# Hybrid convolution and pooling block on eight cores: norms of x in another order, a scrap buffer for their squares, and four multiplications by the norm vector on GpSimd

## The chip, the cores and the metric

The program runs on the 8 cores of one Trainium2 chip. Each core works alone on 2048 of the 16384 tokens (four sequences of 4096, two cores to a sequence) and on 32 tokens ahead of them, the halo; no core waits for another, though all read the same memory. The metric is the device time in microseconds (us) of the slowest core. Engines are named as the profile names them: PE (TensorE, matmuls), DVE (VectorE), ACT (ScalarE), POOL (GpSimd), SP (SyncE, which here only issues DMAs).

## The reference

Per token, with D = 1024 channels and all in float32:

```
u = rms_norm(x, mix_pre_g);  proj = u @ w_in                     # 1024 -> 5120
a, gate, p, g_conv, g_pool = split of proj in five
y_conv = silu(layer_norm(conv31(a * sigmoid(gate)))) @ w_conv_out # depthwise, causal
y_pool = (per_group_linear(pool(p), pool_w) * pool_scale) @ w_pool_out
h  = x + rms_norm((sigmoid(g_conv) * y_conv + sigmoid(g_pool) * y_pool) @ w_o, mix_post_g)
out = h + rms_norm(square(relu(rms_norm(h, mlp_pre_g) @ w_ff1)) @ w_ff2, mlp_post_g)
```

`pool` is, in each of four groups of 256 channels, a trailing mean over 2, 4, 8 or 16 tokens less the token itself. `rms_norm(x, g)` is x * rsqrt(mean(x*x) + eps) * g: a sum of squares per token, one factor per token, and a multiplication by the vector g.

## The kernel before

The kernel writes its instructions down in one fixed order, each onto the queue of its engine; every engine works its queue off in that order. A recording class (`KB`) notes which buffer each instruction reads and writes and puts semaphore waits where an instruction on another engine, or a DMA, has to be finished first. Nothing is reordered afterwards: an instruction that waits holds everything behind it on its engine.

**First stage, x and the pooling projection.** x comes in 16 tiles of 128 tokens (0 to 15) and the halo (-1), each 512 KB in float32, loaded by SP into nine staging buffers. `x_norm(j)`, written (nrm, j) in the list, normalises tile j: ACT squares it and sums along the row (`Square`, 128x1024; its by-product, the squares themselves, goes to the place where the normalised tile is going to lie, one of four buffers `xb`), ACT takes the root, DVE the reciprocal (L401), and DVE multiplies x by the factor and by the norm vector `gb0` in one SCALAR_TENSOR_TENSOR (L250, 128x1024, "STT" below) into bf16. Tiles 0 to 7 are then transposed on PE (`x_tr`, L223, eight 128x128 pieces, and DVE copies them from PSUM, L256, 128x8x128); tiles 8 to 15 by a DMA transpose that SP issues (`DTR`, L263). `p_unit(cc, u)`, written (pu, cc, u), is one group of 8 matmuls with 256 columns: channel chunk cc of the pooling projection for the tokens of tiles 2u and 2u+1; ACT (or DVE, for odd cc and u above 1) copies the result out of PSUM. The list in `do([...])` sets the order of all of these on all engines. After it come 16 groups with 512 columns (`p_group`) for tiles 8 to 11 and then 12 to 15, and the pooling itself on DVE, piece by piece. `wg_load` (POOL) fetches the weights of the next stage into slots 2 and 3 of the weight area, which hold nothing before that.

**Second stage, the gated convolution input.** Four quarters q, each with eight steps rp. A step `glu_pair(q, rp)` has 16 matmuls of 512 columns, a sigmoid on ACT and a multiplication on DVE (L241, 128x2x32x8). Beside them run the convolution's steps for the quarter before, in a cycle of four: three times `cv_w` on DVE (L246, 128x48x16, eight pieces in all, which write the one weight buffer `Wc`), then `cv_mm` on PE, 48 matmuls that read `Wc`, with two DVE additions. At the end of quarter 1 SP issues the load of `poolwT` (the group weights of the pooling branch, 1 MB) once the transposes of that quarter have ended (`cev[1]`). `weff_scale` multiplies it by `pool_scale` on DVE in eight instructions (L246, 128x256) at the end of quarter 2, and `weff_group` in quarter 3 multiplies the result with `w_pool_out` on PE. `pump(n)` takes up to n background tasks from a queue; the only ones in it in quarter 3 are 16 statistics (`BN_STATS`, L610) on DVE.

**Later stages** (gates, output projection, the MLP) take about 720 us and are not touched.

Of the kernel before, what the change touches and what calls it, by code (L numbers as in the profile page):

```python
# [7 lines left out]
F32 = mybir.dt.float32  # L8
BF16 = mybir.dt.bfloat16
AF = mybir.ActivationFunctionType  # L10
ALU = mybir.AluOpType
# [17 lines left out]
RW = TP + TP_N  # L29
SLOT = 4096  # L30
# [140 lines left out]
def build_program():  # L171
# [20 lines left out]
    with ExitStack() as es:  # L192
# [14 lines left out]
        def av(off, *dims, dt=BF16):  # L207
            n = int(np.prod(dims))
            v = arena[:, off:off + (n if dt is BF16 else 2 * n)]
            if dt is not BF16:  # L210
                v = v.bitcast(dt)
            if len(dims) > 1:
                names = ["d%d" % i for i in range(len(dims))]
                v = v.rearrange("p (" + " ".join(names) + ") -> p " + " ".join(names),
                                **{a: d for a, d in zip(names[:-1], dims)})
            return v
# [23 lines left out]
        def TTE(eng, o, a, b, op):  # L240
            kb.op(eng, lambda e: e.tensor_tensor(out=o, in0=a, in1=b, op=op), [a, b], [o])  # L241
# [6 lines left out]
        def STT(o, a, s, b, op0, op1):  # L248
            rd = [a, b] + ([] if isinstance(s, float) else [s])
            kb.op("dve", lambda e: e.scalar_tensor_tensor(out=o, in0=a, scalar=s, in1=b, op0=op0, op1=op1), rd, [o])  # L250
# [42 lines left out]
        c8 = lambda v: v.rearrange("p (k t) -> p k t", k=8)  # L293
        xst = [c8(av(o, 1024, dt=F32)) for o in (RW + 6 * SLOT, RW + 6 * SLOT + 2048, RW + 7 * SLOT, RS, RW + 4 * SLOT + 4192)]
        xst += [z[:, :, 1024 + 256 * i:1280 + 256 * i].bitcast(F32) for i in range(4)]
        gb0 = av(RW + 7 * SLOT + 2048, 1024, dt=F32)
        xb = [av(TP + 3584, 1024), av(TP + 4608, 1024), av(RS + 2048, 1024), av(RW + 4 * SLOT + 3168, 1024)]
        sig = [av(TP + 4160, 512, dt=F32), av(TP + 5184, 512, dt=F32)]
        s2b = [av(RW + 4 * SLOT + i * 1056, 528, dt=F32) for i in range(3)]
        identf = av(RW + 4 * SLOT + 2304, 128, dt=F32)  # L300
# [102 lines left out]
        def rstd(ssq_src, P, epsc, junk, eng):  # L403
            a, r = col()
            ACT(junk, ssq_src, AF.Square, scale=1.0 / 32, accum=a[:P])
            rsqrt(r[:P], a[:P], epsc, eng)
            return r[:P]
# [6 lines left out]
        def x_norm(j):  # L414
            i = x_order.index(j)
            P = 32 if j < 0 else 128
            src, dst = xst[x_buf[i]][:P], c8(xb[i % 4])[:P]
            r = rstd(src, P, 0, dst, "act")
            STT(dst, src, r, c8(gb0)[:P], ALU.mult, ALU.mult)
            if j >= 8:  # L420
                tev[j] = DTR(uT[:, :, H + 128 * j:H + 128 * (j + 1)], xb[i % 4])
            for n in range(9, len(x_order)):
                if x_buf[n] == x_buf[i] and n > i and x_order[n] not in xev:
                    x_load(x_order[n])
                    break
# [14 lines left out]
        def pump(n):  # L440
            for _ in range(n):
                if bgd:
                    bgd.popleft()()
# [74 lines left out]
        nrm, trn, pu, pg = x_norm, x_tr, p_unit, lambda cc, blk: p_group(cc, blk * 512, 512)  # L518
# [5 lines left out]
        def pads():  # L524
# [3 lines left out]
        do([(warm, 6), (nrm, 2), (setup,), (nrm, 3), (trn, 2), (warm, 3), (nrm, 0), (trn, 3), (nrm, 1), (nrm, -1), (warm, 14),  # L528
            (pu, 0, 1), (pu, 1, 1), (trn, 0), (trn, 1), (trn, -1), (pads,), (pu, 2, 1), (pu, 3, 1),
            (pu, 0, 0), (pu, 1, 0), (pu, 2, 0), (pu, 3, 0), (pu, 4, 1), (pu, 4, 0), (nrm, 4), (pu, 5, 1), (pu, 5, 0),  # L530
            (nrm, 5), (pu, 6, 1), (pu, 6, 0), (pu, 7, 1), (trn, 4), (pu, 7, 0), (trn, 5), (nrm, 6),
            (pu, 0, 2), (pu, 1, 2), (pu, 2, 2), (nrm, 7), (trn, 6), (pu, 3, 2), (pu, 4, 2), (nrm, 8), (pu, 5, 2),
            (trn, 7), (pu, 6, 2), (nrm, 9), (pu, 7, 2), (pu, 0, 3), (nrm, 10), (pu, 1, 3), (pu, 2, 3), (nrm, 11),
            (pu, 3, 3), (pu, 4, 3), (nrm, 12), (pu, 5, 3), (nrm, 13), (pu, 6, 3), (nrm, 14), (wg_load, 0), (pu, 7, 3),
            (nrm, 15), (wg_load, 1)])
        for blk in range(2):
            for cc in range(8):
                pq(cc, blk)
# [96 lines left out]
            for hh in range(2):  # L635
                WLOAD(wpo[hh], wpo_v[:, :, hh * 512:(hh + 1) * 512], after=[cev[1]])

        def weff_scale():
            for g in range(4):
                for jc in range(2):  # L640
                    if g == 0:
                        TS(pwT[:, g, jc, :], pwf[:, g, jc, :], vcol(16, 2 * g + jc), ALU.mult, 0.5, ALU.mult)
                    else:
                        TS(pwT[:, g, jc, :], pwf[:, g, jc, :], vcol(16, 2 * g + jc), ALU.mult)
# [11 lines left out]
        for q in range(4):  # L656
            glu_halo(q)
            steps = deque(conv_steps(q - 1) if q else [])
            for rp in range(8):
                glu_pair(q, rp)  # L660
                if steps:
                    steps.popleft()()
                pool_pump(1)
                pump(3)
                if q == 3 and rp % 2 == 0:
                    weff_group(rp // 2)
            conv_in(q)
            if q + 2 < 4:
                wg_load(q + 2)
            if q == 1:  # L670
                pool_pump(32)
                weff_prep()
            if q == 2:
                weff_scale()
                WLOAD(wgp, w_in_v[:, :, 4096:5120], after=[cev[2]])
            if q == 2:
                for r in range(16):
                    bgd.append(lambda r=r: ln_stat(0, r))
# [318 lines left out]
```

How the kernel before makes its waits and increments, by code:

```python
            def body(h, items=items):  # L156
                for waits, fn, ev, dma in items:
                    for sk, v in waits.items():
                        h.wait_ge(sems[sk], rank[sk][v] if sk in rank else v)
                    if fn is None:
                        continue
                    inst = fn(h)
                    if dma:
                        inst.then_inc(sems[ev[0]], 16)
                    elif ev[1] in rank[ev[0]]:
                        inst.then_inc(sems[ev[0]], 1)
```

## Time and profile before

| | us |
|---|---|
| median of 3 runs | 969.09 (968.52 to 1033.9) |
| the profiled execution | 967.8 |
| span of its slowest core (core 0), on which all rows below stand unless another core is named | 966.3 |
| spans of the other cores | 962.9 to 966.2 |
| PE busy in that span | 937.5 |
| DVE, ACT, POOL busy | 451.8, 287.9, 62.5 |
| TensorE's granted clock, mean | 0.997 of full |

The span runs from the first to the last instruction on the core; what the time has beyond it (1.5 us) is start and end. "Idle before, releaser" in a row is how long the engine had nothing to do before the row's first instruction, and which event ended it. A row that merges several instructions says how many (x24) and gives the time from the first start to the last end.

### The profile page before, as it was taken

What the parts mean: (1) busy time and instruction counts of PE and PEld (TensorE: products, weight loads), DVE (VectorE), ACT (ScalarE), POOL (GpSimd) and SP (SyncE); (2) the same over time, 40 slices, a digit from 0 to 9 for tenths busy, and PEclk for the clock granted to TensorE, in tenths of its full rate; (3) what the DMA queues carried; (4) which work ended last, traced back from release to release, by engine and by line L of the source; (5) the groups of instructions that cost most, each with busy time, mean ns of one, the idle gap of its engine ahead of it and who ended that gap; (6) DMA issues with size and microseconds to landing.
All of it is one profiled execution on the core that took longest, in us unless ns stands there. A gap on an engine that the chain in (4) does not pass through costs nothing.

```text
span 966.3 us, 13780 instructions; the slowest of 8 cores (962.9 to 966.3 us)
## 1 busy us (share of the span) xinstructions
PE 937.5 (97%) x4758; PEld 477.7 (49%) x4843; DVE 451.8 (47%) x767; ACT 287.9 (30%) x523; POOL 62.5 (6%) x112
## 2 busy tenths in 40 slices
PE   8889999999999999999999999999999999999996
PEld 4655666665544444444444444444444444444444
DVE  5478786575482134565666620444213431244222
ACT  4553111132115922333335520233112321133211
POOL 1010001000010000121222100000000000000000
PEclk9999999999999999999999999999999999999998
DMA  9986165966894623578879993310022001210021
GB/s 181 256 137 88 27 80 106 144 99 105 116 145 73 123 89 49 128 149 199 154 185 184 211 181 58 131 44 1 1 88 88 1 1 44 88 43 1 1 87 66
DMA packets 109750, 95.39 MB, mean 99 GB/s; under 512 B 60241, under 2 KB 91217, under 8 KB 109554
## 3 DMA queue, kind: packets, MB, share of 16 engines
q0 software_dynamic: 32416, 35.13, 26.4%
q1 hardware_dynamic: 77266, 59.38, 23.5%
q8 instruction: 40, 0.66, 0.3%
q14 instruction: 28, 0.23, 0.1%
HBM read 98.88 MB, written 16.84 MB: 120 GB/s over the span
## 4 chain that ended last, share of the span: by engine, by line
PE 90%; DMA 3%; DVE 2%; ACT 2%; issue 2%; DVEq 0%; ACTq 0%; SPq 0%
PE ps L220 90%; ACT arena L238 2%; DMA arena<-w_in 2%; DMA arena<-xh 1%; DVE arena L241 1%; DVE arena L246 1%; DVE arena L250 0%; PE ps L223 0%; DVE arena L478 0%; ACT sm L238 0%; ACTq L159 0%; DVEq L159 0%; DVE ps L241 0%; DVE arena L256 0%; DVEq L192 0%
## 5 line engine op out<-in xcount | busy, mean ns | idle before, releaser
L220 PE MATMUL ps<-arena 128*128 128x512 bf16 (+4 forms) x4646 | 931.4, 360 | 17.8 <-ACT arena L238 4.7
L220 PEld LDWEIGHTS ps<-arena 128*128 128x128 bf16 (+1 forms) x4731 | 470.6, 103 | 473.8 <-issue 24.5
L238 ACT ACTIVATE arena<-ps 128x512 bf16<-128x512 f32 (+5 forms) x346 | 202.8, 593 | 606.0 <-PE ps L220 450.4
L246 DVE TENSOR_SCALAR ps<-ps 128x512 f32<-128x512 f32 x128 | 89.1, 699 | 110.9 <-PE ps L220 110.3
L241 DVE TENSOR_TENSOR ps<-ps,arena 128x512 f32<-128x512 f32 (+1 forms) x65 | 43.6, 688 | 177.2 <-ACT arena L238 176.7
L250 DVE SCALAR_TENSOR_TENSOR arena<-arena,ps 128x512 bf16<-128x512 f32 (+1 forms) x64 | 43.7, 686 | 126.1 <-ACT arena L238 126.1
L241 DVE TENSOR_TENSOR arena<-ps,arena 128x512 bf16<-128x512 f32 (+2 forms) x52 | 42.3, 830 | 35.5 <-ACT arena L238 29.4
L238 ACT ACTIVATE arena<-arena 128x1024 bf16<-128x1024 f32 (+1 forms) x33 | 34.8, 1054 | 44.6 <-DVE arena L250 35.8
L250 DVE SCALAR_TENSOR_TENSOR arena<-ps,sm,arena 128x512 f32<-128x512 f32 (+1 forms) x65 | 45.1, 737 | 4.1 <-DVE sm L401 3.3
L250 DVE SCALAR_TENSOR_TENSOR arena<-arena,sm 128x1024 bf16<-128x1024 f32 (+1 forms) x33 | 42.3, 1282 | 4.3 <-POOL sm L397 2.4
L241 DVE TENSOR_TENSOR arena<-arena 128x512 bf16<-128x512 f32 (+2 forms) x56 | 38.4, 690 | 4.3
L238 ACT ACTIVATE arena<-arena,vec 128x2048 bf16<-128x2048 bf16 x8 | 31.3, 3918 | 1.7 <-DMA arena<-arena 1.7
L246 DVE TENSOR_SCALAR arena<-arena,vec 128x768 bf16<-128x768 bf16 (+1 forms) x72 | 28.2, 420 | 2.7
L266 POOL DMA_DIRECT2D arena<-w_in x14 | 12.6, 908 | 157.6 <-DMA arena<-arena 138.1
L266 POOL DMA_DIRECT2D arena<-w_ff x16 | 13.5, 851 | 99.5 <-PE ps L220 92.4
L610 DVE BATCH_NORM_STATS2 bnst<-arena 128x6 f32<-128x512 bf16 x32 | 19.9, 680 | 0.0
L397 POOL TENSOR_TENSOR sm<-sm,mhalf 128x1 f32<-128x1 f32 x32 | 18.1, 567 | 5.0 <-POOL sm L396 0.4
L401 DVE RECIPROCAL sm<-sm 128x1 f32<-128x1 f32 (+1 forms) x33 | 5.3, 162 | 27.2 <-ACT sm L238 16.4
L250 DVE SCALAR_TENSOR_TENSOR arena<-arena 128x512 bf16<-128x512 f32 x24 | 16.5, 687 | 1.2
L478 DVE TENSOR_TENSOR_SCAN arena<-arena,scr 128x512 f32<-128x512 f32 x12 | 15.3, 1278 | 2.3 <-ACT arena L238 2.3
L396 POOL TENSOR_SCALAR sm<-sm 128x1 f32<-128x1 f32 x32 | 7.1, 221 | 133.0 <-DVE sm L241 67.6
L238 ACT ACTIVATE sm<-sm,epst 128x1 f32<-128x1 f32 (+1 forms) x33 | 9.7, 295 | 16.1 <-DVE sm L241 14.5
(34 smaller groups left out, 90.8 us busy)
## 6 DMA issues: line engine op xcount, KB each, us to landing
arena<-xh SPq DMA_DIRECT2D x32, 512.0 KB, 8.3
arena<-w_ff POOLq DMA_DIRECT2D x16, 1024.0 KB, 27.4
out<-arena SPq DMA_DIRECT2D x31, 512.0 KB, 2.9
arena<-out SPq DMA_DIRECT2D x16, 512.0 KB, 4.1
arena<-w_in POOLq DMA_DIRECT2D x12, 512.0 KB, 14.4
arena<-w_in POOLq DMA_DIRECT2D x2, 2048.0 KB, 17.9
arena<-gb SPq DMA_DIRECT2D x4, 512.0 KB, 7.0
arena<-w_pool_out POOLq DMA_DIRECT2D x2, 1024.0 KB, 23.7
```

Source lines behind the costliest of these rows:

```text
L220: kb.op("pe", lambda e: e.matmul(o, lhsT=l, rhs=r, start=start, stop=stop), [l, r], [o])
L238: kb.op("act", lambda e: e.activation(out=o, in_=i, func=func, **kw), rd, wr)
L241: kb.op(eng, lambda e: e.tensor_tensor(out=o, in0=a, in1=b, op=op), [a, b], [o])
L246: kb.op("dve", lambda e: e.tensor_scalar(out=o, in0=a, scalar1=s1, scalar2=s2, op0=op0, **kw), rd, [o])
L250: kb.op("dve", lambda e: e.scalar_tensor_tensor(out=o, in0=a, scalar=s, in1=b, op0=op0, op1=op1), rd, [o])
L266: return kb.op("pool", lambda e: e.dma_start(out=o, in_=src), [], [o], dma=True, after=after)
L396: kb.op("pool", lambda e: e.tensor_scalar(out=o, in0=i, scalar1=EPS[epsc], scalar2=None, op0=ALU.add), [i], [o])
L397: kb.op("pool", lambda e: e.tensor_tensor(out=o, in0=o, in1=mhalf[:, 0:n], op=ALU.pow), [o, mhalf[:, 0:n]], [o])
L401: kb.op("dve", lambda e: e.reciprocal(o, o), [o], [o])
L478: kb.op("dve", lambda e: e.tensor_tensor_scan(so, pc[:, lo:lo + n], pc[:, lo - w:lo - w + n], init, ALU.add, ALU.subtract), rd, [so])
L610: kb.op("dve", lambda e: e.bn_stats(o, i), [i], [o])
```

## The change

`x_norm` writes the squares to two scrap buffers `junk` in slot 2 of the weight area, no longer to the place of the normalised tile. For tiles 8, 10, 12 and 14 POOL multiplies x by `gb0` into one of two float32 buffers `xgs` (slots 2 and 3), and DVE multiplies that by the factor per token with a TENSOR_SCALAR. The list has (nrm, 6) to (nrm, 15) one to three entries earlier, and the two `wg_load` behind the last group. `weff_scale` takes a group: its eight instructions move from the end of quarter 2 into steps 1, 3, 5 and 7 of that quarter, two each. `pump(3)` becomes `pump(2)`.

```diff
+        junk = [av(RW + 2 * SLOT + i * 1024, 1024) for i in range(2)]
+        xgs = [c8(av(RW + 2 * SLOT + 2048 + i * 2048, 1024, dt=F32)) for i in range(2)]
...
             src, dst = xst[x_buf[i]][:P], c8(xb[i % 4])[:P]
-            r = rstd(src, P, 0, dst, "act")
-            STT(dst, src, r, c8(gb0)[:P], ALU.mult, ALU.mult)
+            if j in (8, 10, 12, 14):
+                xg = xgs[j // 2 % 2]
+                TTE("pool", xg, src, c8(gb0), ALU.mult)
+                TS(dst, xg, rstd(src, P, 0, c8(junk[i % 2]), "act"), ALU.mult)
+            else:
+                STT(dst, src, rstd(src, P, 0, c8(junk[i % 2])[:P], "act"), c8(gb0)[:P], ALU.mult, ALU.mult)
...
-            (nrm, 5), (pu, 6, 1), (pu, 6, 0), (pu, 7, 1), (trn, 4), (pu, 7, 0), (trn, 5), (nrm, 6),
-            (pu, 0, 2), (pu, 1, 2), (pu, 2, 2), (nrm, 7), (trn, 6), (pu, 3, 2), (pu, 4, 2), (nrm, 8), (pu, 5, 2),
-            (trn, 7), (pu, 6, 2), (nrm, 9), (pu, 7, 2), (pu, 0, 3), (nrm, 10), (pu, 1, 3), (pu, 2, 3), (nrm, 11),
-            (pu, 3, 3), (pu, 4, 3), (nrm, 12), (pu, 5, 3), (nrm, 13), (pu, 6, 3), (nrm, 14), (wg_load, 0), (pu, 7, 3),
-            (nrm, 15), (wg_load, 1)])
+            (nrm, 5), (pu, 6, 1), (pu, 6, 0), (pu, 7, 1), (trn, 4), (nrm, 6), (pu, 7, 0), (trn, 5),
+            (pu, 0, 2), (nrm, 7), (pu, 1, 2), (trn, 6), (pu, 2, 2), (nrm, 8), (pu, 3, 2), (pu, 4, 2), (trn, 7), (nrm, 9), (pu, 5, 2),
+            (pu, 6, 2), (nrm, 10), (pu, 7, 2), (pu, 0, 3), (nrm, 11), (pu, 1, 3), (nrm, 12), (pu, 2, 3), (pu, 3, 3), (nrm, 13),
+            (pu, 4, 3), (pu, 5, 3), (nrm, 14), (pu, 6, 3), (nrm, 15), (pu, 7, 3), (wg_load, 0), (wg_load, 1)])
...
-        def weff_scale():
-            for g in range(4):
+        def weff_scale(g):
...
                 pool_pump(1)
-                pump(3)
+                if q == 2 and rp % 2 == 1:
+                    weff_scale(rp // 2)
+                pump(2)
...
             if q == 2:
-                weff_scale()
                 WLOAD(wgp, w_in_v[:, :, 4096:5120], after=[cev[2]])
```

The order on DVE in the first stage, from the STT of tile 5 to the copy of tile 6's transposes (128x1024 is a norm's multiplication, 128x8x128 the copy of a tile's transposes out of PSUM, 128x256 that of a group of matmuls). Before:

```order
L250 SCALAR_TENSOR_TENSOR arena<-arena,sm 128x1024
L256 COPY arena<-ps 128x8x128 x2
L401 RECIPROCAL sm<-sm 128x1
L250 SCALAR_TENSOR_TENSOR arena<-arena,sm 128x1024
L256 COPY arena<-ps 128x256
```

Now:

```order
L250 SCALAR_TENSOR_TENSOR arena<-arena,sm 128x1024
L256 COPY arena<-ps 128x8x128
L403 RECIPROCAL sm<-sm 128x1
L250 SCALAR_TENSOR_TENSOR arena<-arena,sm 128x1024
L256 COPY arena<-ps 128x8x128
```

The copies of tiles 4 and 5 stood next to each other; now the STT of tile 6 stands between them, ahead of the copy of tile 5.

The order on DVE in quarter 2 of the second stage, steps rp = 1 to 3 (128x2x32x8 ends a `glu_pair`, 128x48x16 is `cv_w`, 128x16x64 the additions behind `cv_mm`, 128x256 `weff_scale`). Before:

```order
L241 TENSOR_TENSOR arena<-ps,arena 128x2x32x8
L246 TENSOR_SCALAR arena<-arena,vec 128x48x16 x3
L241 TENSOR_TENSOR arena<-ps,arena 128x2x32x8
L246 TENSOR_SCALAR arena<-arena,vec 128x48x16 x2
L241 TENSOR_TENSOR arena<-ps,arena 128x2x32x8
L241 TENSOR_TENSOR arena<-ps,arena 128x16x64 x2
```

Now:

```order
L241 TENSOR_TENSOR arena<-ps,arena 128x2x32x8
L246 TENSOR_SCALAR arena<-arena,vec 128x48x16 x3
L246 TENSOR_SCALAR arena<-arena,vec 128x256 x2
L241 TENSOR_TENSOR arena<-ps,arena 128x2x32x8
L246 TENSOR_SCALAR arena<-arena,vec 128x48x16 x2
L241 TENSOR_TENSOR arena<-ps,arena 128x2x32x8
L241 TENSOR_TENSOR arena<-ps,arena 128x16x64 x2
L246 TENSOR_SCALAR arena<-arena,vec 128x256 x2
```

The first two scalings of `poolwT` now stand in step 1, ahead of the last two `cv_w` for which `cv_mm` waits; before, all eight stood behind step 7.

The order on POOL from the start of the program (w_in is the weight of the first and then of the second stage). Before:

```order
L266 DMA arena<-w_in 128x8x256 x8
L266 DMA arena<-convw 128x768 x2
```

Now:

```order
L266 DMA arena<-w_in 128x8x256 x4
L241 TENSOR_TENSOR arena<-arena 128x1024 x4
L266 DMA arena<-w_in 128x8x256 x4
```

The four multiplications by `gb0` stand ahead of the four loads of `wg_load`.

## Rows read from the trace of the kernel before

**Rows 1.** Busy time by engine in the first stage (us, PE, PEld, DVE, ACT, POOL).

```profile
18.00:60.00 42.00, 34.55 (x322) 28.63 (x324) 22.74 (x42) 24.95 (x61) 0.00 (x0) 1.00 1.00 212
```

**Rows 2.** Timeline of PE, first stage: start, us, what, [idle before, releaser].

```profile
34.84 0.61 PE L223 MATMUL ps<-identb,arena 128*128 128x128 bf16 x8 [1.39 <-ACT arena L238]
...
38.07 2.78 PE L220 MATMUL ps<-arena 128*128 128x256 bf16 x24 [1.05 <-ACT arena L238]
...
44.55 0.61 PE L223 MATMUL ps<-identb,arena 128*128 128x128 bf16 x8 [0.64 <-DVE arena L250]
...
47.99 7.15 PE L220 MATMUL ps<-arena 128*128 128x256 bf16 x64 [1.08 <-ACT sm L238]
58.02 42.29 PE L220 MATMUL ps<-arena 128*128 128x512 bf16 x191 [2.88 <-ACT arena L238]
```

**Rows 3.** Load of tile 8: SP's issue, then size and us from issue to landing.

```profile
30.50 1.30 SPq L259 DMA_DIRECT2D arena<-xh  x1
...
arena<-xh SPq DMA_DIRECT2D x1, 512.0 KB, 7.2
```

**Rows 4.** Timeline of ACT: three evictions; the Squares of tiles 6 and 7.

```profile
34.41 0.92 ACT L238 ACTIVATE arena<-ps 128x256 f32<-128x256 f32 x3
...
36.77 1.05 ACT L238 ACTIVATE arena<-arena 128x1024 bf16<-128x1024 f32 x1
...
41.23 1.05 ACT L238 ACTIVATE arena<-arena 128x1024 bf16<-128x1024 f32 x1
```

**Rows 5.** Timeline of DVE: copy of tile 5's transposes; STTs of tiles 6 and 11.

```profile
37.13 0.69 DVE L256 COPY arena<-ps 128x1024 bf16<-128x1024 bf16 x1 [0.36 <-PE ps L223]
...
38.66 1.28 DVE L250 SCALAR_TENSOR_TENSOR arena<-arena,sm 128x1024 bf16<-128x1024 f32 x1
...
53.09 1.28 DVE L250 SCALAR_TENSOR_TENSOR arena<-arena,sm 128x1024 bf16<-128x1024 f32 x1
```

**Rows 6.** DMA transposes of tiles 8 and 11: issue, and us to landing of each.

```profile
46.88 1.52 SPq L263 DMA_TRANSPOSE arena<-arena  x1
...
54.51 1.23 SPq L263 DMA_TRANSPOSE arena<-arena  x1
...
arena<-arena SPq DMA_TRANSPOSE x1, 6.4
...
arena<-arena SPq DMA_TRANSPOSE x1, 3.1
```

**Rows 7.** Load of poolwT: SP's issue on core 0; landing on cores 0 and 1.

```profile
161.42 0.38 SPq L259 DMA_DIRECT2D arena<-poolwT  x1
...
arena<-poolwT SPq DMA_DIRECT2D x1, 1024.0 KB, 7.2
...
arena<-poolwT SPq DMA_DIRECT2D x1, 1024.0 KB, 5.2
```

**Rows 8.** Timeline of DVE, quarter 2: step 1, cv_w in step 2, weff_scale.

```profile
161.57 0.69 DVE L241 TENSOR_TENSOR arena<-ps,arena 128x512 bf16<-128x512 f32 x1 [1.58 <-ACT arena L238]
162.18 1.75 DVE L246 TENSOR_SCALAR arena<-arena,vec 128x768 bf16<-128x768 bf16 x3
...
165.63 0.94 DVE L246 TENSOR_SCALAR arena<-arena,vec 128x768 bf16<-128x768 bf16 x2
...
188.20 2.18 DVE L246 TENSOR_SCALAR arena<-arena,vec 128x256 bf16<-128x256 f32 x8
```

**Rows 9.** Chain that ended last, quarter 2: last matmuls of step 3 before cv_mm.

```profile
164.60 2.98 PE ps L220 x13
```

**Rows 10.** POOL: groups by shape (xcount | busy us, mean ns); an issue in quarter 2.

```profile
L396 POOL TENSOR_SCALAR sm<-sm 128x1 f32<-128x1 f32 x32 | 7.1, 221 | 133.0 <-DVE sm L241 67.6 <-ACT arena L238 65.3
...
L397 POOL TENSOR_TENSOR lnr<-lnr,mhalf 128x16 f32<-128x16 f32 x1 | 2.9, 2942 | 0.1
...
L396 POOL TENSOR_SCALAR lnr<-bnag 128x16 f32<-128x16 f32 x1 | 0.3, 269 | 20.0 <-DVE bnag L705 20.0
...
161.92 1.85 POOL L266 DMA_DIRECT2D arena<-w_in  x2 [12.15 <-DMA arena<-arena]
```

## The prediction, made before the changed kernel had run

> **What bounds the kernel now.** The table of the page comes first: PE is busy 937.5 of 966.3 us, so 28.8 us are all that any reordering can win. The busy time by stretch then says where to look. From 18 to 60 us PE works 34.55 of 42.00 us [rows 1], so a quarter of all the idle time lies in the stretch whose list is rewritten. PE's timeline splits that up: waits of 1.39, 1.05, 0.64, 1.08 and 2.88 us, together 7.04 [rows 2]. The reader should see what each is for, which the releaser named does not always say. At 34.84 PE waits for the norm of tile 4. At 38.07 it waits for DVE's copy of tile 5's transposes, which ends at 37.13 + 0.69 = 37.82 [rows 5]. At 44.55 it waits for the norm of tile 7, at 47.99 for the copy of that tile's transposes. At 58.02 the releaser is given as ACT, but the first group of 512 columns reads tiles 8 to 11, and the DMA transpose of tile 11 lands at 54.51 + 3.1 = 57.61 [rows 6]: 0.41 us later PE starts. In quarter 2 of the second stage PE has no wait that matters; there the views to read are DVE's timeline and SP's, because an instruction is moved there ahead of others.
>
> **First part: the list of the first stage.** Tile 4's norm stays where it is, so the 1.39 us stay. Tile 6's moves up, past the last eviction of (pu, 7, 0) and past the copy of tile 5's transposes. Its Square now follows the three evictions that end at 34.41 + 0.92 = 35.33, instead of starting at 36.77; from a Square to its STT are 38.66 - 36.77 = 1.89 us [rows 4, 5]. So the STT of tile 6 starts at 37.2 and ends at 38.5. The copy of tile 5, ready at 37.13 before, now stands behind it: 38.5 to 39.2. PE started 0.25 us after the copy, so it resumes at 39.4 instead of 38.07: **1.3 us lost**.
>
> From 38.07 to 47.99 + 7.15 = 55.14 PE worked 17.07 us less the two waits of 0.64 and 1.08, that is 15.35 [rows 2]. Both waits go. The Square of tile 7 follows the eviction of (pu, 0, 2): 39.4, a group of 0.93 (2.78 / 3 [rows 2]), about 0.6 for the copy out of PSUM: 41.0, hardly before the 41.23 of rows 4. Its STT ends near 44.2, and PE comes to tile 7's transposes only at 44.55 - 0.64 + 1.3 = 45.2. The copy of these transposes stood behind the STT of tile 8, now stands ahead of the STT of tile 9, and is done by 47; PE wants it at 47.99 - 1.72 + 1.3 = 47.6. So PE reaches the groups of 512 columns at 39.4 + 15.35 = 54.8, and what ends last is again the transpose of tile 11. The Square of tile 11 follows the eviction of (pu, 0, 3): 47.6 + 0.9 + 0.65 = 49.2. The STT is at 51.1 to 52.4, the transpose is issued at 52.5, lands at 55.6 if it takes 3.1 us, and PE starts at 56.0. That is one end. The other: the transpose of tile 8 took 6.4 us and landed at 53.3 [rows 6] because loads of x were still coming in; the next three, now issued closer together, can follow only as fast as SP issues them, 1.23 us each, and the last lands at 57.0, PE at 57.4. I take 56.4, nearer to the first, since tile 11's issue, at 52.5, comes 5.6 us after 46.88, more than 3 x 1.23. **Gain 1.6 us, between 0.6 and 2.0.**
>
> **Second part: POOL's four multiplications.** No row shows a plain two-operand multiplication on POOL. From above, the power of 128x16 took 2.942 us, which for 1024 elements would be 188 us; from below, 128x16 with one tensor took 0.269 us. Nearest is the slope of that simple operation, (0.269 - 0.221) / 15 = 3.2 ns an element [rows 10], so 3.5 us each, an estimate. The Trainium skill (GPSIMD Engine Reference, Elementwise — side-by-side cycle accounting) measures 4497 ns for an addition of 2048 elements, by which it would be 2.25 us and the sum would be the same. Tile 8 lands at 30.50 + 7.2 = 37.7 [rows 3]; its product is wanted near 45, tile 10's near 49, tile 14's near 56. So up to 4.5 us each is covered. DVE's remaining TENSOR_SCALAR costs between 0.27 us (the 128x256 of rows 8) and the 1.28 of an STT; up to 1 us is saved on each of four, off PE's path but for tiles 8 and 10. The scrap buffers take away ACT's wait for the old contents of `xb`; the same wait moves to DVE, for the transpose of four tiles before, which costs PE nothing, since those STTs only feed transposes needed eight groups, 14.2 us, later. `wg_load` stands behind the multiplications on POOL, but waits for the transpose of tile 13 anyway: nothing.
>
> **Third part: weff_scale.** The first two of its eight scalings move from behind step 7 into step 1 of quarter 2. The load of `poolwT` is issued by SP at 161.42 and lands 7.2 us later, at 168.62 [rows 7]; before, its first reader ran at 188.20 and never waited. In step 1 DVE is through with `cv_w` at 162.18 + 1.75 = 163.93 [rows 8]. Now it **waits there 4.7 us** for the load, and an in-order engine holds everything behind: the scalings (2 x 2.18 / 8 = 0.55), the multiplication of step 2 (0.61) and the two last `cv_w` (0.94). These end at 170.7 and PE can start `cv_mm` at 171.0, where it started at 164.60 + 2.98 = 167.6 [rows 9]. **Cost 3.4 us**, and PE, busy almost all of the rest, cannot win it back. Everything here moves with PE, the load included, since the load is released by the transposes at the end of quarter 1; the gain of the first part does not change the gap. The lower end is none; with the 5.2 us that the load takes on core 1 [rows 7] it would be 1.4. The upper is the forecast's own, unless the load slows down further. I take 3.4, since the slowest core sets the time. The other six scalings find the load landed. What leaves the end of quarter 2 (2.18 us of DVE) had PE work beside it: nothing. `pump(2)` for `pump(3)` gives the sixteen statistics 8 x 2 places instead of 8 x 3, just enough: nothing.
>
> **Sum.** Against the profiled execution: 967.8 - 1.6 + 3.4 = 969.6. The median of the runs stands 1.3 above that execution, so **970.9**: no change by the 2% (19.4 us) that a measurement of this kernel can tell. Its own range, from the ends of the first part: 970.5 to 971.9.
>
> **The rivals.**
> - *The load of poolwT comes early enough.* For it: 5.2 us on core 1. Against: 7.2 on core 0, the slowest. With 1.4 us the time is 968.9, with no wait 967.5. Chance 0.24, of which 0.04 for 966.2, where PE does not lose the 1.3 us at the copy of tile 5 either.
> - *POOL and DVE get in each other's way.* Beside POOL's DMA issues at 161.92, three `cv_w` on DVE took 1.75 us where two took 0.94 [rows 8, 10], so 0.3 more than their share. If each multiplication on POOL takes turns with the STT beside it, the STTs of tiles 6 and 11, both on PE's path, take 1.2 us more each: the transpose of tile 11 lands at 58.0, PE starts at 58.4, and the time is 967.8 + 0.4 + 3.4 + 1.3 = 972.9. If the STT waits out a multiplication of 3.5 us, it is 5 us instead of 2.4, and 975.5. Chance 0.18. The Trainium skill (GPSIMD Engine Reference, Specifications) has POOL share its SBUF interfaces with DVE, with contention for DVE instructions with two SBUF inputs, as an STT is; the row of `cv_w` agrees for a one-input instruction, and none shows an STT beside a multiplication.
> - *POOL's multiplication is slow enough to be the bound: slower.* PE wants tiles 12 to 15 eight groups of eight matmuls after 56.4, at 56.4 + 64 x 42.29 / 191 = 70.6 [rows 2]. With T us each the fourth product is there at 37.7 + 4T, the last transpose some 5.5 us later. PE waits for it from T = 6.8 on, and the kernel is slower by 2% (17.6 us more than in my sum) from T = 11.3. For it: the power's 184 ns an element. Against: the simple operation's 3.2. Chance 0.02.
> - *The norms do not follow the loads.* Tile 8 had landed at 37.7, yet tile 7's Square still stands behind an eviction that PE releases near 41. This is in my sum; if the transposes' queue takes the rest, the gain is 0.6 and the time 971.9.
>
> **How the numbers follow.** Forecast 0.55; load early 0.24; contention 0.18; slow POOL 0.02; something else 0.01. From 967.2 to 974.5 the range holds the forecast, most of the first rival and two thirds of the second. Faster by over 2% needs two thirds of all idle time: 0.01. Slower by over 2% is POOL's rival: 0.02. Within: 0.97.
>
> **What would show it.** On PE: the wait near 38 grows to 2.4, those near 44 and 48 go, the first group of 512 columns starts near 56.4. On DVE: a wait of 4 to 5 us for the load of `poolwT` in step 1 of quarter 2; on PE, 3 us before `cv_mm` near 169. POOL: four rows of 2 to 4.5 us. Without DVE's wait the third part is wrong; with STTs over 1.5 us beside POOL, the second.

## The result, and the profile after

The changed kernel takes **975.65 us** (median of 4 runs, 973.32 to 995.71; the kernel before 968.81 beside it). The ratio is 1.0065 with a 95% interval of [1.0041, 1.0089]: 0.65% or 6.3 us slower, which is more than the measurement is uncertain, though less than 2%. The prediction had 970.9 and a range to 974.5. The profiled execution took 975.57 us. One run of each of the two kernels (995.71 and 1033.9) fell into a second, slower state of the chip; all ratios, and the medians under the experiments, leave such runs out.

The cores fall apart. The marks in this table are the sigmoids of the 32 halo tokens that open each quarter of the second stage (a 32x256 row on ACT): the first mark ends the first stage, and from the third to the fourth is quarter 2. The waits are those of DVE for the load of `poolwT` and of PE before the next `cv_mm`; the clock is the granted one, in the slices of 5 us named.

| core | span before / after | first mark before / after | quarter 2 before / after | DVE / PE wait | clock 170-175, 175-180 |
|---|---|---|---|---|---|
| 0 | 966.3 / 966.0 | 88.97 / 89.78 | 34.98 / 36.3 | 2.42 / 1.15 | 1.00, 1.00 |
| 1 | 964.3 / 973.6 | 88.88 / 92.10 | 34.98 / 40.9 | 5.85 / 4.16 | 1.00, .66 |
| 2 | 966.2 / 965.7 | 90.57 / 89.50 | 34.99 / 36.4 | 2.54 / 1.24 | 1.00, 1.00 |
| 3 | 964.0 / 974.0 | 88.89 / 92.52 | 34.98 / 41.2 | 4.54 / 3.42 | .83, .50 |
| 4 | 964.2 / 971.3 | 89.38 / 92.52 | 34.98 / 38.8 | 5.34 / 3.66 | 1.00, 1.00 |
| 5 | 962.9 / 968.1 | 87.89 / 91.39 | 34.99 / 36.5 | 2.48 / 1.37 | 1.00, 1.00 |
| 6 | 965.2 / 972.5 | 89.71 / 90.98 | 34.98 / 41.0 | 5.37 / 4.26 | .98, .68 |
| 7 | 964.6 / 972.2 | 88.83 / 90.59 | 34.98 / 40.9 | 5.74 / 4.15 | .88, .78 |

Core 3, now the slowest, lost 10.0 us: 3.6 in the first stage (88.89 to 92.52), 6.25 in quarter 2, and 0.2 in quarter 1. The change has two costs where a gain and a smaller cost were forecast.

**The first stage on core 3.** PE (start, us, what, [idle before, releaser]), the rows that answer to [rows 2]:

```profile
35.22 0.68 PE L223 MATMUL ps<-identb,arena 128*128 128x128 bf16 x8 [0.47 <-ACT arena L238]
38.08 1.91 PE L220 MATMUL ps<-arena 128*128 128x256 bf16 x16 [2.18 <-DVE arena L256]
...
45.04 0.61 PE L223 MATMUL ps<-identb,arena 128*128 128x128 bf16 x8 [1.99 <-ACT sm L238]
45.49 9.77 PE L220 MATMUL ps<-arena 128*128 128x256 bf16 x88
58.72 11.65 PE L220 MATMUL ps<-arena 128*128 128x512 bf16 x41 [3.46 <-DMA arena<-arena]
```

The wait near 38 grew to 2.18 and the one near 48 went, both as forecast. But the one near 44 is longer, 1.99, and the 512-column groups start at 58.72 instead of the forecast 56.4 (on this core they started at 56.24 before). The reason stands in POOL's and DVE's timelines of the same core:

```profile
41.35 2.35 POOL L241 TENSOR_TENSOR arena<-arena 128x1024 f32<-128x1024 f32 x1 [1.20 <-DMA arena<-xh]
46.79 2.36 POOL L241 TENSOR_TENSOR arena<-arena 128x1024 f32<-128x1024 f32 x1 [3.09 <-DVE arena L246]
51.65 2.36 POOL L241 TENSOR_TENSOR arena<-arena 128x1024 f32<-128x1024 f32 x1 [2.49 <-DVE arena L246]
```

```profile
35.94 1.28 DVE L250 SCALAR_TENSOR_TENSOR arena<-arena,sm 128x1024 bf16<-128x1024 f32 x1
...
41.39 3.40 DVE L250 SCALAR_TENSOR_TENSOR arena<-arena,sm 128x1024 bf16<-128x1024 f32 x1
...
47.75 2.49 DVE L250 SCALAR_TENSOR_TENSOR arena<-arena,sm 128x1024 bf16<-128x1024 f32 x1
...
50.75 0.75 DVE L246 TENSOR_SCALAR arena<-arena,sm 128x1024 bf16<-128x1024 f32 x1
51.42 0.42 DVE L256 COPY arena<-ps 128x256 f32<-128x256 f32 x1
...
52.01 3.08 DVE L250 SCALAR_TENSOR_TENSOR arena<-arena,sm 128x1024 bf16<-128x1024 f32 x1
```

An STT with no multiplication beside it still takes 1.28 us, as in [rows 5]. The three that overlap one (tiles 7, 9 and 11) take 3.40, 2.49 and 3.08, and each ends 1.08 or 1.09 us after POOL does (44.79 against 43.70, 50.24 against 49.15, 55.09 against 54.01): nearly its whole length lies behind POOL's. POOL's first multiplication, from 37.79 to 40.14, has no STT beside it. Over the cores the STT of tile 9 takes 2.48 to 2.78 and that of tile 11 3.08 or 3.09; that of tile 7 is back at 1.29 on core 7, where it starts ahead of the multiplication. The STT of tile 7 makes PE wait at 45.04, that of tile 11 delays the last transpose. The Trainium skill (GPSIMD Engine Reference, Specifications) has such contention for DVE instructions with two SBUF inputs; the trace agrees, and has the size: 1.2 to 2.1 us more for each. The wait goes both ways, and the one that starts second has it. On core 6 POOL's first multiplication starts while an STT runs; the STT keeps its 1.28, and the multiplication takes 3.12 (POOL, then DVE):

```profile
36.39 3.12 POOL L241 TENSOR_TENSOR arena<-arena 128x1024 f32<-128x1024 f32 x1 [30.86 <-DMA arena<-xh]
```

```profile
36.02 1.28 DVE L250 SCALAR_TENSOR_TENSOR arena<-arena,sm 128x1024 bf16<-128x1024 f32 x1
```

**The clock behind that wait, and quarter 2.** Busy time by engine on core 3 (us, PE, PEld, DVE, ACT, POOL, granted clock, DMA share, GB/s), before and then after:

```profile
55.00:85.00 30.00, 28.76 (x127) 12.76 (x128) 23.70 (x46) 11.55 (x21) 3.50 (x4) 0.94 0.83 126
150.00:190.00 40.00, 40.00 (x275) 27.67 (x273) 23.78 (x43) 5.53 (x10) 4.70 (x6) 1.00 0.96 148
```

```profile
55.00:85.00 30.00, 26.54 (x113) 11.37 (x111) 21.57 (x46) 10.13 (x20) 3.56 (x4) 0.89 0.91 132
150.00:190.00 40.00, 36.14 (x225) 25.55 (x224) 22.73 (x42) 4.56 (x8) 4.66 (x6) 0.91 0.85 132
```

Of core 3's 3.6 us in the first stage, 2.5 are the later start of the 512-column groups and 1.1 come behind it, where the clock over 55 to 85 us was 0.94 and is 0.89. In 150 to 190 us PE now stands idle for 3.86 us, where before it never did, and its clock falls to 0.91. Closer, the load of `poolwT` (SP's issue and its time to landing), then DVE, then PE behind it, all on core 3:

```profile
164.81 0.38 SPq L259 DMA_DIRECT2D arena<-poolwT  x1
...
DMA to landing us min/median/max: 7.2/7.2/7.2
```

```profile
165.69 1.95 DVE L246 TENSOR_SCALAR arena<-arena,vec 128x768 bf16<-128x768 bf16 x3
172.18 0.62 DVE L246 TENSOR_SCALAR arena<-arena,vec 128x256 bf16<-128x256 f32 x2 [4.54 <-DMA arena<-poolwT]
172.71 0.68 DVE L241 TENSOR_TENSOR arena<-ps,arena 128x512 bf16<-128x512 f32 x1
173.31 0.94 DVE L246 TENSOR_SCALAR arena<-arena,vec 128x768 bf16<-128x768 bf16 x2
```

```profile
174.50 7.68 PE L220 MATMUL ps<-arena 128*128 128x128 bf16 x58 [3.42 <-DVE arena L246]
```

Landing at 164.81 + 7.2 = 172.0, a wait of 4.54 on DVE, of 3.42 on PE: the forecast was 4.7 and 3.4. What the forecast lacked comes after it. The clock of three slices, from the wait on:

```profile
170.00:175.00 5.00, 1.58 (x11) 0.97 (x10) 2.56 (x6) 0.60 (x1) 0.20 (x1) 0.83 1.18 191
175.00:180.00 5.00, 5.00 (x46) 4.74 (x45) 1.34 (x2) 0.00 (x0) 0.36 (x1) 0.50 1.25 140
180.00:185.00 5.00, 5.00 (x24) 3.36 (x23) 2.25 (x5) 0.60 (x1) 0.00 (x0) 0.99 1.20 164
```

PE comes back and works a whole slice at 0.50, the lower of its two levels (1.2 of 2.4 GHz). Half the work of 5 us is 2.5 us; with 3.42 of waiting and about 0.3 (an estimate) for the 0.5 us that PE had worked before 175, at 0.50 too, that makes the 6.25. The table shows it on every core: quarter 2 is longer than 34.98 by the PE wait and 0.2 more where the clock stays at 1.00 (cores 0, 2, 4, 5), and by the wait and 1.8 more on cores 1, 6 and 7, 2.8 on core 3, where it falls. Only on core 3 does it fall while PE still waits; on cores 1, 6 and 7 it falls some 0.6 to 1.1 us after PE has come back. On core 1 PE resumes at 174.87, still has 0.99 in the first of these slices, and works the next three us at 0.50:

```profile
175.00:176.00 1.00, 1.00 (x21) 1.00 (x20) 0.22 (x1) 0.00 (x0) 0.56 (x1) 0.99 1.25 140
176.00:179.00 3.00, 3.00 (x32) 3.00 (x30) 1.23 (x1) 0.00 (x0) 0.00 (x0) 0.50 1.20 126
```

The Trainium skill (TensorE: Matmul & The Clock Gate, HAM oscillation — how this bites in real kernels) tells of matmuls that restart at the half clock after a wait for a DMA; the trace agrees on core 3 and, with that delay, on cores 1, 6 and 7, while core 4, with a wait of 3.66 us, kept its clock.

### The profile page after: what moved, and what is told of

Its sections match the earlier page's. It is cut to its first block, busy times and chain, and to the rows that moved or that the text cites. A ratio compares the mean times of both kernels' runs of the same rounds, so it can differ in the third digit from the quotient of the medians.

```text
span 974.0 us, 13877 instructions; the slowest of 8 cores (965.7 to 974.0 us)
## 1 busy us (share of the span) xinstructions
PE 944.8 (97%) x4843; PEld 479.5 (49%) x4843; DVE 454.5 (47%) x767; ACT 287.8 (30%) x523; POOL 71.8 (7%) x116
## 4 chain that ended last, share of the span: by engine, by line
PE 89%; DMA 5%; DVE 3%; issue 1%; ACT 1%; DVEq 0%; POOL 0%; ACTq 0%; SPq 0%
PE ps L220 89%; DMA arena<-w_in 2%; DMA arena<-xh 1%; DVE arena L246 1%; DMA arena<-arena 1%; ACT arena L238 1%; DMA arena<-poolwT 1%; DVE arena L250 1%; DVE arena L484 0%; DVE arena L241 0%; PE ps L223 0%; ACT sm L238 0%; DVE arena L256 0%; POOL arena L266 0%; DVEq L159 0%
```

## The experiments

Ratios are to the kernel before, run on the same chip beside each, with 95% intervals. "First mark" is that of the table; means are over the eight cores of one profiled execution.

**a1_weff_back: the change without its third part.**

```diff
-                if q == 2 and rp % 2 == 1:
-                    weff_scale(rp // 2)
...
             if q == 2:
+                for g in range(4):
+                    weff_scale(g)
```

> The change with weff_scale back at the end of quarter 2; list, scrap buffers and POOL's multiplications stay. Theory of two losses: DVE does not wait for poolwT, so PE has no wait in quarter 2 and its granted clock stays at 1.00 there; quarter 2 takes 35.0 us on every core, as before (36.3 to 41.2 with the change). The first stage stays late: first group of 512 columns at 58 to 59.7, STTs of tiles 7, 9 and 11 at 2.5 to 3.4 us. Time about 971 (968.8 + 2 to 3). Rival, that the first stage's lateness is what makes the second stage lose (the load of poolwT or the clock suffers from it): quarter 2 stays at 36 to 41 us and the time near 975.

Measured 1.0019 [1.0004, 1.0033]; profiled 969.86. Quarter 2 is back at 35.0 us on all cores and the clock there at 1.00, so the moved scalings are the whole of what was lost in quarter 2. The first stage stays as in the change: the 512-column groups start at 58.3 to 59.4, the first mark is 91.15 on the mean (before 89.14).

**a2_no_pool_mult: the change without POOL's multiplications** (tiles 8, 10, 12, 14 by STT like the others).

```diff
-            if j in (8, 10, 12, 14):
+            if j in ():
```

> The change without POOL's four multiplications (all tiles by the STT); list, scrap buffers and the moved weff_scale stay. Theory of two losses: all STTs take 1.28 us again, the transpose of tile 11 lands near 56 and the first group of 512 columns starts at 56.4, 2 us earlier than with the change; quarter 2 still takes 36 to 41 us. Time about 972 (975.6 less 2 to 4, the more where the clock also stays up after the shorter wait). Rival, that the list itself makes the first stage late (tile 6's norm ahead of the copy of tile 5): the first group stays at 58 or later and the time at 975.

Measured 1.0046 [1.0029, 1.0063], median 972.2. All STTs take 1.28 or 1.29 again, on every core; the one of tile 11 on core 3:

```profile
49.70 1.28 DVE L250 SCALAR_TENSOR_TENSOR arena<-arena,sm 128x1024 bf16<-128x1024 f32 x1
```

The 512-column groups start at 54.9 to 57.5 and the first mark comes at 86.0 to 89.5, so the late start was POOL's doing. Quarter 2 takes 36.5 to 41.1 us as in the change; the clock fell on cores 0 and 6 this time, not on 1, 3, 6 and 7.

**a3_weff_alone: the kernel before, with the third part only.**

```diff
+                if q == 2 and rp % 2 == 1:
+                    weff_scale(rp // 2)
...
-                weff_scale()
```

> The kernel before with nothing but weff_scale moved into steps 1, 3, 5 and 7 of quarter 2. Theory of two losses: first stage as before, quarter 2 at 36 to 41 us instead of 35.0, with a wait of PE of 1 to 4 us before cv_mm and on some cores half the granted clock behind it. Time 973 to 974 (968.8 + 5). If the load of poolwT landed late only because the first stage was late: no wait, 968.8.

Measured 1.0063 [1.0045, 1.0081], 973.9 us: as slow as the whole change, from eight small instructions. PE waits 1.4 to 4.1 us. Cores 1, 2 and 5 worked on at a lower clock; here PE on core 2 and two slices of its clock:

```profile
172.65 9.66 PE L220 MATMUL ps<-arena 128*128 128x128 bf16 x68 [3.82 <-DVE arena L246]
```

```profile
170.00:175.00 5.00, 2.35 (x23) 2.38 (x24) 2.56 (x6) 0.00 (x0) 0.56 (x1) 0.61 1.21 137
175.00:180.00 5.00, 5.00 (x39) 4.20 (x37) 2.97 (x4) 0.00 (x0) 0.00 (x0) 0.71 1.20 158
```

Core 2's quarter 2 takes 41.5 us: 34.98, 3.8 of waiting, 2.7 more.

**b3_fill_the_wait: a3, with 14 matmuls of 512 columns whose result nothing reads in front of the `cv_mm` that waits.** If the lower clock is a cost of its own, added work in the wait should win it back.

```diff
             if cc == 2:
+                b = banks(2)
+                for _ in range(14):
+                    MM(ps[:, b, :], uT[:, 0, H:H + 128], uT[:, 0, H:H + 512], True, True)
...
```

> The kernel before with weff_scale moved into steps 1, 3, 5 and 7 (as a3_weff_alone), and 14 matmuls of 512 columns, 3.0 us, whose result nobody reads, in front of the cv_mm that waits. PE then does not stand still for more than about 1 us there. Theory that the granted clock falls because PE stood still for 3.3 us and more: clock 1.00 in quarter 2 on all cores, quarter 2 at 38.0 us where the wait was shorter than 3.0 and 38.4 to 39.1 where it was 3.4 to 4.1, time 972 (974.2 with the wait empty), although work was added. Rival, that the clock falls for another reason (the loads running beside it): some cores at half the clock as in a3_weff_alone, quarter 2 up to 41 us, time 974.

Measured 1.0048 [1.0034, 1.0062], 972.4: 3.0 us more work on PE (quarter 2 takes 38.0 on cores 1, 3, 5 and 7, where the wait is covered), and yet no slower than a3; the 1.5 us less by the ratios are not shown, since the two intervals overlap. The clock in quarter 2 is 1.00 on all cores. On cores 0, 2, 4 and 6 PE would have stood still for 3.5 to 5.0 us without the filler (filler and remaining wait together); a2, a3 and the change have twelve unfilled waits of 3.3 us and more in quarter 2, and nine of them were followed by the lower clock. Core 4 has a wait left, behind its filler, and keeps its clock too (PE, then the clock):

```profile
174.05 8.25 PE L220 MATMUL ps<-arena 128*128 128x128 bf16 x72 [2.01 <-DVE arena L246]
```

```profile
175.00:180.00 5.00, 4.94 (x49) 3.93 (x48) 2.97 (x4) 0.00 (x0) 0.02 (x1) 1.00 1.25 151
```

The slowest quarter 2 falls from 41.5 to 40.2 us. So the fall of the clock comes from PE's wait, and is paid on top of it.

**b2_weff_steps_4_to_7: the scalings in the loop, but later** (in b1 below, one group in each of steps 4 to 7).

```diff
+                if q == 2 and rp >= 4:
+                    weff_scale(rp - 4)
```

> As b1_tile6_back, but with weff_scale spread over the steps of quarter 2 as in the change, one group in each of steps 4, 5, 6 and 7 in place of 1, 3, 5 and 7. The load of poolwT lands at 165 to 171, step 4 asks at about 175. Theory that the wait for the load is the whole cost of the move: no wait of DVE or PE, quarter 2 at 35.0 us, granted clock 1.00 there, time as b1_tile6_back within 0.5 us. Rival, that DVE's work in the steps delays cv_w and the multiplications by itself: quarter 2 longer than 35.5 us and the time 1 us or more above b1_tile6_back.

Measured 0.9994 [0.9984, 1.0003]. DVE waits for no load, quarter 2 is 35.0 us and its clock 1.00 on all cores. Interleaving costs nothing; standing ahead of the load costs all of it.

**a4_list_and_scrap: the change without its second and third parts** (new list, scrap buffers, `pump(2)`).

```diff
-            if j in (8, 10, 12, 14):
+            if j in ():
...
-                if q == 2 and rp % 2 == 1:
-                    weff_scale(rp // 2)
...
+                for g in range(4):
+                    weff_scale(g)
```

> The change with weff_scale back at the end of quarter 2 and without POOL's multiplications: what is left is the new list, the scrap buffers and pump(2). By my prediction's first part: 1.3 us lost at the copy of tile 5, both waits near 44 and 48 gone, first group of 512 columns at 56.4, quarter 2 at 35.0; time 967.2 (968.8 - 1.6). Rival, that the list is itself a loss: 970 or more.

Measured 0.9987 [0.9977, 0.9997], 966.5: **faster than both kernels**, by 1.3 us against the kernel before, where 1.6 was forecast. PE on core 0, to be read against [rows 2]:

```profile
38.05 3.51 PE L220 MATMUL ps<-arena 128*128 128x256 bf16 x16 [2.18 <-DVE arena L256]
...
44.97 9.77 PE L220 MATMUL ps<-arena 128*128 128x256 bf16 x88
56.74 13.54 PE L220 MATMUL ps<-arena 128*128 128x512 bf16 x61 [2.00 <-ACT arena L238]
```

The waits near 44 and 48 are gone, the one near 38 is 2.18, the 512-column groups start at 56.74 (55.2 to 57.7 over the cores; forecast 56.4). The first mark is 87.87 on the mean, 1.27 earlier.

The longer wait near 38 has a second cost, for which the forecast has no term. Behind it the same 16 matmuls take 3.51 us on core 0 (above) and 1.91 on core 3:

```profile
38.20 1.91 PE L220 MATMUL ps<-arena 128*128 128x256 bf16 x16 [2.18 <-DVE arena L256]
```

The clock over 37 to 43 us is 0.72 or 0.73 on cores 0, 2 and 4 and 1.00 on the others; in the change it is 0.72 on cores 1, 2, 4, 5 and 6, in the kernel before on core 6 alone. That core 0 starts so near to the forecast is therefore partly chance: it came to the transposes of tile 4, whose place no part of the change moves, at 33.60, and at 34.84 in [rows 2]. Counted from there the 512-column groups start after 22.6 us on the mean over the cores, before after 23.4.

**b1_tile6_back: a4 with the norm of tile 6 back behind (trn, 5)**, to win the 1.3 us at the copy of tile 5.

```diff
-            (nrm, 5), (pu, 6, 1), (pu, 6, 0), (pu, 7, 1), (trn, 4), (nrm, 6), (pu, 7, 0), (trn, 5),
+            (nrm, 5), (pu, 6, 1), (pu, 6, 0), (pu, 7, 1), (trn, 4), (pu, 7, 0), (trn, 5), (nrm, 6),
```

> The list and the scrap buffers alone (POOL's multiplications and the moved weff_scale undone) with tile 6's norm back behind the transposes of tile 5. If the STT of tile 6 ahead of the copy of tile 5 costs PE what the changed kernel shows (a wait of 2.2 us near 38 where it was 1.05), the wait goes back to about 1 us, all that follows in the first stage, paced by PE, is 1.2 us earlier, and the time is 966 (967.0 - 1.2). If the DMA transpose of tile 11 is what ends last whatever PE does before it, PE only waits longer at its first group of 512 columns, and the time stays at 967.

Measured 0.9996 [0.9986, 1.0005], 967.3. The wait near 38 is back at 1.05 us, the clock behind it is 1.00 on all cores, and counted from the transposes of tile 4 the 512-column groups start after 21.4 us, 1.2 sooner than in a4. But PE pays it out there: it still waits for the transpose of tile 11, now 1.8 to 3.5 us, and on five cores (two in a4) the clock of 55 to 85 us is .94 or .95. The first mark is 87.82 on the mean, that of a4 87.87. Core 5:

```profile
37.71 1.91 PE L220 MATMUL ps<-arena 128*128 128x256 bf16 x16 [1.05 <-ACT arena L238]
...
55.41 14.80 PE L220 MATMUL ps<-arena 128*128 128x512 bf16 x60 [2.29 <-DMA arena<-arena]
```

```profile
55.00:85.00 30.00, 29.59 (x129) 12.95 (x130) 23.59 (x46) 9.33 (x18) 3.59 (x5) 0.94 0.87 123
```

**c1_fill_first_stage: b1 with ten unread matmuls of 512 columns in that wait.**

```diff
+            if (cc, t0) == (0, 1024):
+                b = banks(1)
+                for _ in range(10):
+                    MM(ps[:, b, :], uT[:, 0, H:H + 128], uT[:, 0, H:H + 512], True, True)
...
```

> As b1 (967.41, ratio 0.9996), with ten matmuls of 512 columns whose result nothing reads (about 2.2 us at full clock) on PE in front of the first group of 512 columns. In b1 PE waits 1.8 to 3.5 us there and the granted clock of 55 to 85 us is .94 on six cores. Theory (part of the list's gain is lost to the clock that falls after this wait): the ten matmuls lie in the wait, the clock of 55 to 85 us is 1.00 on all cores, halo(0) ends between 86 and 87.5 us on all cores instead of 85.7 to 90.0, and the time is about 966, ratio 0.997 to 0.999. Rival (the clock at 55 to 85 us has another cause, or the fill is simply work that is added): the same clock as b1 and 0 to 2.2 us more, 967.4 to 969.6.

Measured 0.9987 [0.9978, 0.9997], 966.2. The clock of 55 to 85 us is 1.00 on seven cores (in b1 on three; the six with .94 that the expectation names are five), and the first mark comes at 85.4 to 88.2 on those seven; core 3, where 2.37 us of waiting were left, has .94 and 89.69. On core 5 PE starts the real work 0.66 us later than in b1 and ends the stage 1.03 us earlier (87.23 against 88.26). That fits the theory, though it is one profiled execution of each; that the time is lower than b1's is not shown, since the intervals overlap. Core 5 again:

```profile
56.07 14.19 PE L220 MATMUL ps<-arena 128*128 128x512 bf16 x65 [1.13 <-DMA arena<-arena]
```

```profile
55.00:85.00 30.00, 28.93 (x134) 13.07 (x135) 24.04 (x47) 9.64 (x17) 4.61 (x6) 1.00 0.83 125
```

**c2_norms_earlier: b1 with the norms of tiles 7 to 11 earlier still.**

```diff
-            (pu, 0, 2), (nrm, 7), (pu, 1, 2), (trn, 6), (pu, 2, 2), (nrm, 8), (pu, 3, 2), ...
+            (nrm, 7), (pu, 0, 2), (pu, 1, 2), (trn, 6), (nrm, 8), (pu, 2, 2), (pu, 3, 2), ...
```

> As b1, with the norms of tiles 7 to 11 one or two groups of matmuls earlier still. Theory (the first group of 512 columns waits for the transpose of tile 11, whose issue follows its norm): the group starts 1 to 2 us earlier than in b1, and the time is 966 to 966.5. Rival (the loads of x and the transposes' queue limit the transposes, not the norms): the group starts where it does in b1, within 0.5 us on the median core, and the time is that of b1, 967.4.

Measured 0.9991 [0.9982, 1.0001], 966.3. The 512-column groups start at 54.7 to 56.3, in b1 at 54.2 to 57.2, with a median that is the same within 0.2. The rival holds: nothing is to be seen of a gain from moving these norms further.

**b4_all_eight_on_pool: a1 with tiles 8 to 15 all multiplied on POOL.** No STT is left beside a multiplication then, only TENSOR_SCALARs, which read one tensor. I expected these to be spared; the rival had every DVE instruction on SBUF wait.

```diff
-            if j in (8, 10, 12, 14):
-                xg = xgs[j // 2 % 2]
+            if j >= 8:
+                xg = xgs[j % 2]
```

> The change with weff_scale back at the end of quarter 2 and all of tiles 8 to 15 multiplied by the norm vector on POOL, so that behind tile 7 no STT runs beside a multiplication, only the TENSOR_SCALAR with one tensor input. Theory that only an instruction with two SBUF inputs waits out POOL's multiplication: TENSOR_SCALAR 0.75 us throughout, STT of tile 7 at 2 to 3.4 us (the only one), first group of 512 columns at 57, time 968 (between a4_list_and_scrap's 967.0 and a1_weff_back's 969.9). Rival, that every DVE instruction on SBUF waits, the one-input ones too: TENSOR_SCALAR at 1.5 to 3 us, first group at 59 or later, time 970 or more.

Measured 1.0035 [1.0018, 1.0053]. **My theory fell.** POOL and then DVE on core 6:

```profile
52.61 2.37 POOL L241 TENSOR_TENSOR arena<-arena 128x1024 f32<-128x1024 f32 x1 [0.70 <-DVE arena L246]
```

```profile
45.61 0.75 DVE L246 TENSOR_SCALAR arena<-arena,sm 128x1024 bf16<-128x1024 f32 x1
...
52.39 0.41 DVE L256 COPY arena<-ps 128x256 f32<-128x256 f32 x1
...
52.98 2.55 DVE L246 TENSOR_SCALAR arena<-arena,sm 128x1024 bf16<-128x1024 f32 x1
55.45 0.41 DVE L256 COPY arena<-ps 128x256 f32<-128x256 f32 x1
```

A TENSOR_SCALAR of 0.75 us takes 2.55 beside POOL and ends 0.55 after it. The copies out of PSUM keep 0.41, beside POOL or not. The change has one such on core 7, of 1.66 us. The Trainium skill (GPSIMD Engine Reference, Specifications) names, beside DVE instructions with two SBUF inputs, those that run in a mode with two ports. That this TENSOR_SCALAR runs in one would fit its 0.75 us against the STT's 1.28; no row names the mode.

**c3_scrap_alone: the kernel before with the scrap buffers only.** The first `wg_load` still stands ahead of the norms of tiles 14 and 15, so their squares overwrite weights that the next stage multiplies with.

```diff
+        junk = [av(RW + 2 * SLOT + i * 1024, 1024) for i in range(2)]
...
-            r = rstd(src, P, 0, dst, "act")
-            STT(dst, src, r, c8(gb0)[:P], ALU.mult, ALU.mult)
+            STT(dst, src, rstd(src, P, 0, c8(junk[i % 2])[:P], "act"), c8(gb0)[:P], ALU.mult, ALU.mult)
```

> The kernel before with one thing of the change: the squares' by-product goes to the two scrap buffers. Theory (ACT's wait for the old contents moves to DVE and neither is on PE's path): no change, ratio 0.999 to 1.001. Rival (ACT's wait did hold a tile's norm on PE's path): 1 us faster or more, ratio under 0.999.

A miss by my own edit: its profiled spans are 970 to 977 us and no ratio is drawn from it. ACT's square of tile 14 waits for the weights to land in its scrap buffer, and PE then waits 6.49 us for the transposes of the last tiles (core 0, ACT, then PE):

```profile
72.87 1.06 ACT L238 ACTIVATE arena<-arena 128x1024 bf16<-128x1024 f32 x1 [15.67 <-DMA arena<-w_in]
```

```profile
79.60 25.62 PE L220 MATMUL ps<-arena 128*128 128x512 bf16 x105 [6.49 <-DMA arena<-arena]
```

It shows why the change has the two loads behind the last norm.

**c4_scrap_loads_behind: c3 with the two loads there.**

```diff
-            (pu, 3, 3), (pu, 4, 3), (nrm, 12), (pu, 5, 3), (nrm, 13), (pu, 6, 3), (nrm, 14), (wg_load, 0), (pu, 7, 3),
-            (nrm, 15), (wg_load, 1)])
+            (pu, 3, 3), (pu, 4, 3), (nrm, 12), (pu, 5, 3), (nrm, 13), (pu, 6, 3), (nrm, 14), (pu, 7, 3),
+            (nrm, 15), (wg_load, 0), (wg_load, 1)])
```

> The kernel before with the two scrap buffers, and the two loads of the next stage's weights behind the last norm, as the change has them (in c3 the first of them stood ahead of the norms of tiles 14 and 15, whose squares went into the slots that it fills, and the end of the first halo moved from 88 to 91 us to 95 to 102 us). Theory (the scrap buffers and the place of the loads are off PE's path): the first halo ends between 87.5 and 91 us as before, and the time is that of before, ratio 0.999 to 1.001. Rival (the loads come later and the next stage waits for its weights): the first halo ends 2 us or more later and the ratio is 1.002 or more.

Measured 1.0006 [0.9996, 1.0016]: no change. The gain of a4 is the list's; `pump(2)`, which a4 has too, acts only behind the first stage.

## Why the prediction was wrong

By the ratios, times 968: list and buffers -1.3 us (a4), POOL's multiplications +3.1 (a1 less a4), the scalings +4.5 (change less a1) to +6.1 (a3 alone). With 4.5 the sum is the measured 6.3 because it is a chain of differences; with 6.1, the only price of the scalings that does not come from the change itself, it is 7.9, and the gap is within the intervals. The forecast had -1.6, 0 and +3.4, with 1.3 us on top for the median.

- **First part, right in its waits and near in its size, with a term missing.** The longer wait at the copy of tile 5 (2.18, 1.1 us more where 1.3 was forecast), the vanished waits near 44 and 48, a start at 56.4 (55.2 to 57.7) and a gain of 1.6 (1.3) are all seen in a4, where beside the list only the buffers, the place of the two loads (c4 has both) and `pump(2)` differ. What the sum put at nothing is the clock behind the longer wait: 3.51 us instead of 1.91 for 16 matmuls on core 0. That the gain came out so close is in part luck.
- **Second part, wrong: this step failed.** "Covered" was checked for POOL's own work, and there it held: 2.35 us each (3.5 assumed). But the STTs beside it were taken at 1.28 us. They wait POOL out, and with that the first part's gain turned into a loss of 2.0 (first mark, a1 against before, on the mean). Against a4 that is 3.3 us: 2.4 by which the 512-column groups start later (58.8 against 56.3 on the mean), and 0.9 behind, where the clock of 55 to 85 us is below 1.00 on six cores, in a4 on two. It is the contention rival's second variant, a wait and not turns, given 0.18 together with the first; a row of 0.3 us beside DMA issues was the only evidence in the trace, and it says nothing of an instruction that streams two tensors for 2.4 us. That this variant's 975.5 is close to the measured 975.65 is luck: it rests on an STT of 5 us, measured are at most 3.40, and it has no lower clock.
- **Third part, right in mechanism and wait, too small in price: this term was mis-sized.** 4.54 and 3.42 us, on core 3, are the forecast's 4.7 and 3.4; over the cores PE waits 1.15 to 4.26. The sum took PE to come back as fast as it had been; on four of eight cores it worked at half clock behind the wait, 1.8 to 2.8 us more. The kernel before shows the same price in its first stage: PE waits 2.63 to 2.88 us before its 512-column groups on every core, and the clock over 55 to 85 us is .94 on four of them (2, 3, 4 and 7; 2.66 us on core 3). The forecast looked at core 0, which has 1.00 there, and at a stretch that ends at 60 us [rows 1].
- **Which core counts.** The slowest is the maximum over eight. A wait that hits one core by 1.2 us and another by 4.3 is priced by the second. The forecast did take core 0's 7.2 us of load rather than core 1's 5.2 for that reason, rightly: loads of 5.1 to 8.0 us occurred.
- **The scrap buffers and `pump(2)` cost nothing**, as forecast. For the buffers c4 shows it; `pump(2)` was not undone by itself, but on cores 0 and 3 the convolution's norm on POOL comes 91.3 us after the mark of quarter 3 in the change as before.

## What to carry to other kernels

DVE work moved to POOL need not run in parallel with DVE's other work on SBUF. For the two forms measured here, STT and TENSOR_SCALAR beside a multiplication on POOL, count the one that starts second as waiting for the first, and place POOL's work beside copies out of PSUM or beside nothing. Before an instruction is moved forward in an in-order queue, compare its new place with the landing of what it reads, on the core where that lands last. Price a wait of PE not by its length alone but with the clock after it, even where it only grows from 1.05 to 2.2 us, and look on all cores for rows that show that price.

## What the runs showed of the hardware that was not expected

- An STT of 1.28 us takes 2.49 to 3.40 beside a POOL multiplication of 2.35 and ends 1.08 us after it; a one-tensor TENSOR_SCALAR of 0.75 takes 2.55 and ends 0.55 after it; copies out of PSUM keep their 0.41. Where the STT is the first to start it keeps its 1.28, and POOL's multiplication takes 3.12.
- Matmuls that nothing reads, put into a wait, can keep the clock up without costing time: with 3.0 us of them it stayed at 1.00 in quarter 2 of b3, and the kernel was no slower than a3.
- The lower clock also followed waits that are shorter than those of quarter 2: 2.18 us near 38 on core 0 of a4, 2.29 us on core 5 of b1. On cores 1, 6 and 7 of the change it fell some 0.6 to 1.1 us after PE had come back.
- Which cores lose their clock changes from run to run (1, 3, 6, 7 in the change; 0 and 6 in a2; 1, 2, 5 in a3), and a wait of 3.66 us left it at 1.00 on one core where 3.42 halved it on another. What decides between them stays open.
